# Experts of a mixed layer: three quarters of the down projection in high and low parts, weights in other pieces, a third buffer of result rows, first block split in quarters

## What is computed

```python
def route(x2, router_w, router_bias):
    ...
    return idx, gw                      # 8 experts of each row and their weights

    def one_block(args):
        rows, gates, e = args
        xb = x_pad[rows]
        h = jax.nn.silu(xb @ w_gate[e]) * (xb @ w_up[e])      # 1024 -> 256
        return (h @ w_down[e]) * gates[:, None].astype(xb.dtype)   # 256 -> 1024
...
    ffn = shared + routed_experts(x2, idx, gw, ...)
    y = layer_norm(DN_ALPHA * h1 + ffn.reshape(h1.shape), ln2_g, ln2_b)
```

## Time and profile before

| | us |
|---|---|
| median of three runs (1666.99 to 1671.74) | 1669.2 |
| the profiled execution | 1664.48 |
| its span, first to last instruction | 1662.7 |
| expert_stage, from the first rows read by PE to the last scatter | 911.9 to 1567.1 |
| of it block 1 to block 62, steady | 929.5 to 1551.4 |
| PE busy over the span | 1513.0 (91%) |
| DVE, ACT, POOL busy | 1027.1, 598.2, 468.4 |
| DMA over the span | 313.21 MB, mean 188 GB/s |

### The profile page before, as it was taken

How to read it: one execution, slowest core, us unless ns; L and a number is a source line. 1 busy time by engine, 2 the same in 40 slices (tenths; PEclk the granted TensorE clock), 3 DMA queues, 4 the chain that set the end, 5 groups by cost and what they waited for, 6 DMA issues and landing times. The chain is left out here.

```text
span 1662.7 us, 21050 instructions
## 1 busy us (share of the span) xinstructions
PE 1513.0 (91%) x8028; PEld 1140.9 (69%) x8028; DVE 1027.1 (62%) x1633; ACT 598.2 (36%) x860; POOL 468.4 (28%) x297
## 2 busy tenths in 40 slices
PE   7999689989899997699998899999999999999664
PEld 7999689988898886344433666777776677767321
DVE  4815998605566575135452777777777777766376
ACT  3346323332303302000001555555555555555201
POOL 2423554422133231003212233332222111232023
PEclk9999789998989997799999899999999999999885
DMA  5222112210000000630034799999999999998393
GB/s 199 77 77 64 51 63 84 82 52 1 1 1 1 1 1 14 248 141 14 26 131 181 289 362 374 376 367 372 372 372 362 365 364 362 362 366 336 115 410 101
DMA packets 53158, 313.21 MB, mean 188 GB/s; under 512 B 14928, under 2 KB 15952, under 8 KB 34320
## 3 DMA queue, kind: packets, MB, share of 16 engines
q1 hardware_dynamic: 33312, 276.16, 43.6%
q0 software_dynamic: 19760, 35.89, 5.8%
HBM read 301.33 MB, written 42.12 MB: 207 GB/s over the span
## 5 line engine op out<-in xcount | busy, mean ns | idle before, releaser
L1856 DVE TENSOR_TENSOR gate_up_lo<-wide,gate_up_hi 128x2048 fp32r<-128x2048 f32 x128 | 293.0, 2290 | 96.1 <-ACT gate_up_hi L1799 94.6
L325 PE MATMUL bank<-x_hi,w_hi 128*128 128x274 f32 x768 | 231.0, 301 | 32.1 <-POOL w_lo L287 23.3
L1799 ACT ACTIVATE gate_up_hi<-wide 128x2048 fp32r<-128x2048 f32 x128 | 244.5, 1913 | 7.4 <-PEq L1195 7.4
L327 PE MATMUL bank<-x_hi,w_lo 128*128 128x274 f32 x768 | 227.8, 297 | 0.0
L326 PE MATMUL bank<-x_lo,w_hi 128*128 128x274 f32 x768 | 227.4, 296 | 0.0
L1727 PE MATMUL bank<-gate_up_hi,rows_hi 128*128 128x512 f32 x512 | 206.4, 403 | 8.0 <-DVE rows_lo L1865 8.0
L1729 PE MATMUL bank<-gate_up_hi,rows_lo 128*128 128x512 f32 x512 | 200.9, 392 | 0.0
L1728 PE MATMUL bank<-gate_up_lo,rows_hi 128*128 128x512 f32 x512 | 200.2, 391 | 0.0
L1665 POOL DMA_INDIRECT expert_rows<-lru,slot_ids x64 | 98.2, 1535 | 332.5 <-DVE lru L1872 317.7
L325 PEld LDWEIGHTS bank<-x_hi,w_hi 128*128 128x128 f32 x768 | 150.4, 196 | 34.5 <-POOL w_lo L287 29.7
L287 POOL TENSOR_TENSOR w_lo<-w_raw,w_hi 128x1024 fp32r<-128x1024 f32 x48 | 119.1, 2483 | 186.9 <-ACT w_hi L388 186.9
(11 more groups left out here) (276 smaller groups left out, 2437.3 us busy)
## 6 DMA issues: line engine op xcount, KB each, us to landing
wide<-in_w_exp SPq DMA_DIRECT2D x64, 2048.0 KB
wide<-in_w_exp SPq DMA_DIRECT2D x43, 1024.0 KB
w_raw<-in_w_in SPq DMA_DIRECT2D x48, 512.0 KB, 3.3
last_down<-in_w_exp SPq DMA_DIRECT2D x21, 1024.0 KB
expert_rows<-expert_rows SPq DMA_DIRECT2D x8, 2048.0 KB, 12.8
wide<-in_w_out SPq DMA_DIRECT2D x1, 3584.0 KB, 22.1
wide<-in_w_out SPq DMA_DIRECT2D x1, 2560.0 KB, 14.0
zt<-in_x_t SPq DMA_DIRECT2D x2, 1096.0 KB, 7.0
```

Of the source, the lines that this page charges most:

```text
L325: nc.tensor.matmul(out, wh[:, k, :], x_hi[:, k, at], start=(k == 0), stop=False)
L327: last = nc.tensor.matmul(out, wl[:, k, :], x_hi[:, k, at], start=False, stop=(k == DC - 1))
L1799: nc.scalar.activation(half(w_hi[b % 2], u), half(w_gu[b % RAW], u), ACT.Copy).then_inc(s_whi, 1)
L1856: nc.vector.tensor_tensor(half(w_lo[b % 2], u), half(w_gu[b % RAW], u), half(w_hi[b % 2], u), ALU.subtract).then_inc(s_wlo, 1)
```

## The change

In expert_stage:

- **Down in high and low parts.** Three of the four units of 128 x 512 down weights (`DN_UNITS`: both units of the left half of the result, and the first of the right half) are split: ACT makes `down_hi` (1536 columns), DVE `down_lo`, ACT `hidden_hi`, DVE `hidden_lo`, and PE takes nine fp32r matmuls for them. The fourth unit stays one float32 matmul with a copy of half of the hidden rows.
- **Who writes results.** ACT writes both halves of a result (write_y); DVE no longer does. The result rows have three buffers (`Y_ROWS`).
- **Order.** DVE makes the second half of gate_up_lo for b+1 (not b+2) just ahead of the first half for b+2. ACT makes hidden_hi and down_hi between write_y and its last split.
- **Loads.** SP issues three DMAs per block: gate/up in 8 KB pieces (main memory now holds the two halves of an expert's gate/up as blocks of their own), the split 3/4 of down in 6 KB pieces (two buffers, free when down_lo of two blocks earlier is made) and the last quarter in 2 KB pieces (three buffers). Gate/up of b+3 is issued behind the down of b.
- **First block.** Its weights are split in four quarters of 1024 columns; the first quarter comes ahead of the rows.

Outside of it: `masks` and `future` move out of `consts` into a tile of their own that is freed after the delta rule (a DMA more at the start, of 512 KB that `consts` loses), the routing's values move from `states` to a tile `routing`, and projection_stage waits for the new load at its end.

```diff
-    sp.dma_start(mem.w_gu[i], expert[:, 0:W_GU]).then_inc(mem.gu_loaded[i], 16)
-    sp.dma_start(mem.w_dn[i], expert[:, W_GU:W_EXP].rearrange("p (c n) -> p c n", c=FC)).then_inc(mem.dn_loaded[i], 16)
+DN_RAW = 2
+DN_WHOLE = D // 2
+DN_SPLIT = FC * D - DN_WHOLE
+DN_UNITS = ((0, 0), (0, 1), (1, 0))
...
+def load_gate_up(sp, mem, dram, b):
+    sp.dma_start(mem.w_gu[b % RAW].rearrange("p (h n) -> p h n", h=2), dram["w_gu"][b].rearrange("h p n -> p h n"))\
+        .then_inc(mem.gu_loaded[b % RAW], 16)
+def load_down(sp, mem, dram, b):
+    sp.dma_start(mem.w_dn[b % DN_RAW], dram["w_dn"][b, :, 0:DN_SPLIT]).then_inc(mem.dn_loaded[b % DN_RAW], 16)
+def load_down_whole(sp, mem, dram, b):
+    sp.dma_start(mem.w_dn_whole[b % RAW], dram["w_dn"][b, :, DN_SPLIT:]).then_inc(mem.dn_whole_loaded[b % RAW], 16)
...
         @block.sync
+            gate_up(RAW)
+            gate_up(RAW + 1)
+            for b in range(DN_RAW, NE):
+                sp.wait_ge(s_dlo, b - DN_RAW + 1)
+                load_down(sp, mem, dram, b)
                 if b >= RAW:
                     sp.wait_ge(s_dn1, b - RAW + 1)
+                    load_down_whole(sp, mem, dram, b)
+                gate_up(b + RAW)
...
             def down(b):
                 pe.wait_ge(s_hdr, b + 1)
-                pe.wait_ge(s_dn_w[b % RAW], 16 * (b // RAW + 1))
+                pe.wait_ge(s_dlo, b + 1)
+                pe.wait_ge(s_dn_whole[b % RAW], 16 * (b // RAW + 1))
...
+                        if (c, n) in DN_UNITS:
+                            nc.tensor.matmul(out, h_hi[:, c, :], d_hi[:, at], start=(c == 0), stop=False)
+                            nc.tensor.matmul(out, h_hi[:, c, :], d_lo[:, at], start=False, stop=False)
+                            last = nc.tensor.matmul(out, h_lo[:, c, :], d_hi[:, at], start=False, stop=(c == FC - 1))
+                        else:
+                            last = nc.tensor.matmul(out, hidden_t[:, c, :], w_dn_whole[b % RAW], start=False, stop=True)
...
         @block.scalar
+            def split_down(b):
+                act.wait_ge(s_dn_w[b % DN_RAW], 16 * (b // DN_RAW + 1))
+                if b:
+                    act.wait_ge(s_dn1, b)
+                nc.scalar.activation(d_hi, w_dn[b % DN_RAW], ACT.Copy).then_inc(s_dhi, 1)
...
+            split_first(0)
+            read_rows(0)
+            for q in range(1, 4):
+                split_first(q)
...
         @block.vector
+            def split_hidden(b):
+                dve.wait_ge(s_hhi, b + 1)
...
+                nc.vector.tensor_tensor(h_lo, turned, h_hi, ALU.subtract)
+                nc.vector.tensor_copy(hidden_t[:, FC - 1, :], turned[:, FC - 1, :]).then_inc(s_hdr, 1)
```

More of the change, by code:

```diff
@@ L67 @@
 _at = 0
-for _name, _n in (("ident", P), ("tri", P), ("before", P), ("ones", P), ("masks", LEVELS * P), ("future", P),
-                  ("experts", NE), ("valid", TILES + 1), ("row", 1), ("ln_eps", 1), ("over", TILES + 1),
+for _name, _n in (("ident", P), ("tri", P), ("before", P), ("ones", P), ("experts", NE), ("valid", TILES + 1), ("row", 1), ("ln_eps", 1), ("over", TILES + 1),
                   ("entries", (TILES + 1) * TOPK * 4)):
@@ L1163, in take @@
             nonlocal at
-            view = mem.carve(mem.states, at, *dims)
+            view = mem.carve(mem.routing, at, *dims)
             at += int(np.prod(dims))
@@ L1593, in expert_stage @@
         rows = mem.rows
-        act_g, hidden = (carve(mem.zt, D * ROWS + FF * i, FF) for i in range(2))
-        hidden_t = carve(mem.zt, D * ROWS + 2 * FF, FC, P)
-        y = [carve(mem.lru, D * i, D) for i in range(2)]
-        x_t = carve(mem.lru, 2 * D, DC, P)
+        y = [carve(mem.lru, D * i, D) for i in range(Y_ROWS)]
+        act_g, hidden = (carve(mem.lru, D * Y_ROWS + FF * i, FF) for i in range(2))
+        hidden_t = carve(mem.lru, D * Y_ROWS + 2 * FF, FC, P)
+        x_t = carve(rows[1], 0, DC, P)
+        h_hi, h_lo = (take(f"hidden_{n}", FC, P, dt=F32R) for n in ("hi", "lo"))
+        d_hi, d_lo = (take(f"down_{n}", DN_SPLIT, dt=F32R) for n in ("hi", "lo"))
         extra_ids = ctx.enter_context(nc.sbuf_tensor("extra_ids", [P, 4], U32))
@@ L1783, in extra @@
                     for c in range(FC):
-                        last = nc.tensor.matmul(mem.bank[4 + n][:, :], hidden_t[:, c, :],
-                                                w_dn[0][:, c, 512 * n:512 * n + 512], start=(c == 0), stop=(c == FC - 1))
+                        unit = FC * c + n
+                        weights = w_dn[0][:, 512 * unit:512 * unit + 512] if (c, n) in DN_UNITS else w_dn_whole[0]
+                        last = nc.tensor.matmul(mem.bank[4 + n][:, :], hidden_t[:, c, :], weights,
+                                                start=(c == 0), stop=(c == FC - 1))
                 last.then_inc(s_xdn, 1)
@@ L1809, in read_rows, with split_first @@
                         .then_inc(s_xhi, 1)
-            def write_y(b):
-                act.wait_ge(s_dn0, b + 1)
-                if b >= 2:
-                    act.wait_ge(s_out[b % 2], 16 * (b // 2))
-                nc.scalar.activation(y[b % 2][:, 0:512], mem.bank[4][:, :], ACT.Copy, scale=weight[:, b, 2:3])\
-                    .then_inc(s_y0, 1)
-            for b in range(2):
-                for u in range(2):
-                    split(b, u)
-                if b == 0:
-                    read_rows(0)
+            def split_first(q):
+                if q == 0:
+                    act.wait_ge(s_gu_w[0], 16)
+                nc.scalar.activation(quarter(w_hi[0], q), quarter(w_gu[0], q), ACT.Copy).then_inc(s_whi, 1)
+            def split_down(b):
[3 more added lines that the diff above has]
+                nc.scalar.activation(d_hi, w_dn[b % DN_RAW], ACT.Copy).then_inc(s_dhi, 1)
+            def write_y(b):
+                if b >= Y_ROWS:
+                    act.wait_ge(s_out[b % Y_ROWS], 16 * (b // Y_ROWS))
+                for n, (ready, done) in enumerate(((s_dn0, s_y0), (s_dn1, s_y1))):
+                    act.wait_ge(ready, b + 1)
+                    nc.scalar.activation(y[b % Y_ROWS][:, 512 * n:512 * n + 512], mem.bank[4 + n][:, :], ACT.Copy,
+                                         scale=weight[:, b, 2:3]).then_inc(done, 1)
+            split_first(0)
+            read_rows(0)
+            for q in range(1, 4):
+                split_first(q)
+            for u in range(2):
+                split(1, u)
             for b in range(NE):
@@ L2063, in constant_tables @@
 def constant_tables():
-    c = np.zeros((P, N_CONSTS), np.float32)
+    c, d = np.zeros((P, N_CONSTS), np.float32), np.zeros((P, N_DELTA_CONSTS), np.float32)
     def put(name, value):
-        at, n = CONSTS[name]
-        c[:, at:at + n] = value
+        table, out = (CONSTS, c) if name in CONSTS else (DELTA_CONSTS, d)
+        at, n = table[name]
+        out[:, at:at + n] = value
     p, q = np.arange(P)[:, None], np.arange(P)[None, :]
```

139 lines of the change are left out of this document (80 added, 59 removed).

## The result

| | before | after |
|---|---|---|
| median, us (lowest to highest) | 1668.1 (1661.84 to 1671.74) | 1688.67 (1684.0 to 1695.07) |
| ratio, with its interval | | 1.0138 (1.0112 to 1.0164) |
| span of the profiled execution | 1662.7 | 1684.1 |
| block, mean of 1 to 62, start of up to start of up | 10.03 | 10.34 |

The forecast was 1642, with a range of 1634 to 1662. The blocks alone cost 62 x (10.34 - 10.03) = 19.4 us more, of a difference of 21.4 us between the spans. The rest is small: the first block gained about 4, the last lost about 5, and the stages on either side differ by 1 to 2.

The account below looks back on a forecast made before the run. PE was taken as the bound, at 10.03 us per block. Terms -26.7 (blocks), -4.15 and +0.5 (first block), +3.0 (last block) sum to -27.3: 1664.48 becomes 1637.2, plus 4.7 for the median gives 1642, range 1634 to 1662.

Parts of the forecast that it names:

- Down on PE: PE's down product per block: 3.00 us instead of 3.43, saving 0.43 per block, 26.7 us over 62 blocks (21 to 32).
- DVE and ACT: Busy time per block of 9.60 us: DVE 8.43 and ACT 8.20, so both keep up with PE.
- Loads: Weight loads per block: gate/up plus 1 MB ahead take 8.4 us, hidden while the DMA carries a block in 9.60.
- rival A: DMA becomes the bound in the blocks: ceiling 382 GB/s, block 9.82 us, 1655.7 us in all; chance 0.25.
- The order on DVE: Gate/up load goes out about 4.7 us after up, needed 16 us later, so it stays hidden.
- First block: Start of the expert stage: weights in quarters let PE start up(0) 4.15 us earlier, with 0.5 given back.
- Last block: End of the expert stage: nothing hides the new chain, a loss of 3.0 us (2.1 to 4.8).
- Third buffer of result rows: ACT's scatter waits (107.4 us in 42 blocks) go: worth nothing by itself, but makes room for ACT's longer chain.
- B: Main memory is already the limit: block stays 10.03 us, only the stage's ends change, 1668.7 us; chance 0.07.
- C: Slower through three loads per block instead of two: block 10.2 us, 1680 us in all; chance 0.08.

Follow-up runs that it names:

- after_spread: The changed kernel with the list of an expert's rows written to even partitions first, then odd, so rows reach over all 128: 1629.53 us, ratio 0.9818.
- after_early_free: The changed kernel, but DVE makes the second half of gate_up_lo(b+2) at the end of block b, as before the change: 1658.29 us, ratio 0.999.
- spread_first_late: The changed kernel with rows spread, but the first block's rows stand behind all four quarters of its weights again: 1636.04 us, ratio 0.9846.
- spread_two_y: The changed kernel with rows spread, but two buffers of result rows instead of three: 1625.49 us, ratio 0.9795.
- before_spread_short: The kernel before with rows spread over all partitions and two of down's four float32 matmuls left out: 1599.08 us, ratio 0.9635.
- before_loads: The kernel before with only the change's loads: gate/up in 8 KB pieces, down as two DMAs of 6 KB and 2 KB pieces: 1662.65 us, ratio 1.0009.
- after_spread_early: The changed kernel with rows spread and the second half of gate_up_lo(b+2) made at the end of block b: 1627.11 us, ratio 0.9796.

## Why the prediction was wrong, point by point

**Down on PE: right, a little undersized.** The forecast was 3.00 us in place of 3.43, and a block of 9.60 where PE sets the pace. The timeline of after_spread, where it does:

```profile
1196.78 0.48 PE L1773 MATMUL bank<-gate_up_hi,rows_hi 128*128 128x512 f32 x1
...
1202.33 1.03 PE L1758 MATMUL bank<-consts,zt 128*128 128x128 f32 x8
1203.12 0.48 PE L1798 MATMUL bank<-down_hi,hidden_hi 128*128 128x512 f32 x1
1203.43 0.40 PE L1799 MATMUL bank<-down_lo,hidden_hi 128*128 128x512 f32 x1
...
1206.13 0.38 PE L1783 MATMUL bank<-consts,lru 128*128 128x128 f32 x2
1206.26 0.48 PE L1773 MATMUL bank<-gate_up_hi,rows_hi 128*128 128x512 f32 x1
```

Down takes 3.01 (1203.12 to 1206.13), and the surplus of its first matmul is there (0.31 to the second, where 0.23 is usual). But the transposes ahead now take 0.79 instead of 0.87, and up 5.55 instead of 5.58. The block is 9.48: 0.54 saved, not 0.43, a little beyond the upper bound of 0.52. The term left out was that the neighbours of down get shorter too.

**DVE and ACT: right.** In after_spread DVE is busy 437.70 / 500 x 9.48 = 8.30 us per block (forecast 8.43) and ACT 415.26 / 500 x 9.48 = 7.87 (8.20). Neither is the bound, and with the DMA out of the way PE never waits for down_lo.

**Loads: this step failed.** It said that a gate/up load of 2 MB and the 1 MB ahead of it need 8.4 us, and that loads "stay hidden as long as the DMA can carry a whole block in 9.60". Both the 8.4 us and rival A's ceiling of 382 GB/s were means over 16 engines. A load is landed when its last part is in, and that was after 15.0 us in the kernel before already. The sign stood in the trace: 0.98 at 374 GB/s in the earlier trace rows, next to 1.00 at 421 where no rows move. The prediction read the gap as load starts with an empty queue, though its own row for such a start, 320 GB/s, has a share of 1.04 and not a low one. What the runs showed in place of the 8.4 us and the 9.60 is this: bunched, the last part of a load came after 20.6 us and the block was 10.34; spread, after 12.2 with 9.48. With PE shortened in the kernel before, the block was 9.91 bunched and 9.11 spread.

**The order on DVE: a second miss, in the same step.** The prediction saw that gate/up goes out 4.7 us after an up and took it for harmless, as 16 us were left until the weights are needed. With the last part at 15 us and more there was next to no slack to give away. The move costs 10.34 against 9.95 us per block (after_early_free), which is what turns "no gain" into a loss. With even engines it is free. The two causes don't add up, since they are one chain: uneven engines make the load long, and a late release makes it start late.

**First block: right.** Before, PE started 7.69 us after ACT. In the changed kernel:

```profile
910.81 1.06 ACT L1868 ACTIVATE gate_up_hi<-wide 128x1024 fp32r<-128x1024 f32 x1 [7.73 <-PEq L1217]
...
914.38 0.80 PE L1772 MATMUL bank<-gate_up_hi,rows_hi 128*128 128x512 f32 x1 [1.61 <-DVE rows_lo L1941]
```

3.57 us, so 4.1 gained, where 4.15 was forecast. spread_first_late is 0.0028 above after_spread in the ratios, 4.7 us, with intervals that overlap; its own trace has 6.98 us in this place, 3.4 more than the changed kernel.

**Last block: inside the bounds, above the middle.** The forecast was a loss of 3.0 (2.1 to 4.8). From the start of the last up to the last scatter before took 15.65 us, now 20.32: 4.7 lost; in after_spread 19.19, 3.5 lost. PE, idle for 4 us as forecast, comes back at half clock (granted 0.50 from 1579 to 1584 us):

```profile
1574.55 0.38 PE L1782 MATMUL bank<-consts,lru 128*128 128x128 f32 x2
1578.97 0.77 PE L1797 MATMUL bank<-down_hi,hidden_hi 128*128 128x512 f32 x1 [4.04 <-issue]
1579.54 0.63 PE L1798 MATMUL bank<-down_lo,hidden_hi 128*128 128x512 f32 x1
1579.96 0.63 PE L1799 MATMUL bank<-down_hi,hidden_lo 128*128 128x512 f32 x1
...
1586.41 0.96 POOL L1708 DMA_INDIRECT expert_rows<-lru,slot_ids  x1 [9.19 <-ACT lru L1881]
```

The matmuls are 0.43 apart instead of 0.23.

**Third buffer of result rows: wrong.** It was called what makes room for ACT's longer chain. spread_two_y runs without it at 0.9795 against 0.9818, the same within the intervals. That is with the rows spread; two buffers were not tried in the changed kernel with the rows bunched, where scatters may land later.

**The rivals.** A had the right engine and the right sign in the profile (ACT waiting for weights, PE idle, share near 1 below 385 GB/s), but its price, 9.82, came from the mean. B, that nothing is gained, is what after_early_free does, though not for B's reason: on the one core at work the kernel moves 388 GB/s as soon as rows are spread, and 391 in before_spread_short, so the 358 GB/s of the Trainium skill ("DMA: Bandwidth & Descriptors", Specifications) are not the limit here. C came out with the right sign and the wrong cause: its third load costs nothing that before_loads can show. A rival that asks how the rows lie on the engines was missing.

With the rows spread the changed kernel reaches 0.9818 of before; on the first chip that would be 0.9818 x 1668.1 = 1638 us (an estimate), close to the 1642 of the forecast. Some of that closeness is luck, since down saved more than forecast and the last block lost more, but apart from the loads the terms of the sum held. What was missing was the one resource that isn't shared evenly.

**What stays open.** The traces don't say which engine carries which row; the 9 and 7 parts are read from the increments, the 10.2 us are worked out for 8 engines, and 4 late parts in after_early_free fit neither number. That the spread helps is shown; whether the engines themselves are full, or something behind them that serves the same partitions, isn't told apart. Why packets get longer is not shown. Why the bunched kernels with the late release have a mean of 10.34 and not 10.0 as the others agrees with the round trip of the buffers (10.8 against 8.9 us from landing to issue), but what the slow engines do in between wasn't looked at. In the first ten blocks the wait is absent because three experts are loaded ahead; how fast that lead is used up wasn't tried.

## What to carry to other kernels

Before shortening the bound engine of a kernel with a DMA share above 0.9, look at when the *last* part of a load lands and not at the mean share or rate; if the last parts come far behind the first, the load per DMA engine may be uneven and the next bound nearer than the mean says. It is worth trying to spread lists of rows that fill only part of the partitions over all of them: it costs a second small DMA and was worth 3.4% here where the loads set the pace, and nothing clear where PE did. When the order of an engine is changed, ask of each moved instruction which buffer it frees and which load waits for that. The best versions here, after_spread_early and spread_two_y, are 2.0% below the kernel before.

## What the runs showed of the hardware

- Gathers and scatters with 68 of 128 rows valid, bunched, left 9 of 16 parts of a 2 MB load landing within 9.1 us and 7 after 16.4 to 20.6 (medians of the complete loads); spread over the partitions, all landed within 12.2 us. Bunching on the upper partitions did the same as on the lower ones.
- The mean DMA share did not tell the two apart: 0.98 at 355 GB/s bunched, 1.00 at 388 spread.
- One core, with no other at work in the kernel, sustained 388 to 391 GB/s over 500 us.
- Rows of 8 KB instead of 16 KB made no difference that could be measured, even with the DMA as the bound (1.0166 and 1.0121, overlapping intervals).
- Eight transposes took 0.87 us up to the start of a float32 group and 0.79 us up to the start of an fp32r group.
- The mean of the 6 KB packets was 0.317 us bunched and 0.239 spread, at the same median of 0.234.
